# One gate-projection slot per attention head, another split of the modulation columns, and 32 bytes of padding

## What is computed

```python
# first block
h = rms_norm(x, g_pre)
mla_in, rwkv_in, z_mla, z_rwkv, gate_mla, gate_rwkv = split(h @ w_in)
q, kv = ...                      # latent projections, rms norm, rotary part
y_mla = mla_attention(q_nope, q_rope, k_nope, k_rope, v_mla)   # 8 heads, softmax over 256 keys
y_rwkv = bidirectional_scan(...)                               # 16 heads = 8 pairs
# each y is multiplied by z * sigmoid(z); then branch projections, gates, w_out, residual
# third block, from the vector c alone
mod = silu(c) @ w_ada + b_ada    # 6 * 2048 values = 96 columns of 128
```

## Time and profile before

| | |
|---|---|
| median of 3 runs | 3726.21 us (3722.5 to 3728.68) |
| the profiled execution's own time | 3726.89 us |
| its span, first to last instruction | 3725.6 us |
| PE busy | 3562.8 us (96%) |
| DVE busy | 2231.9 us (60%) |
| ACT busy | 1407.4 us (38%) |
| mean granted TensorE clock | 0.984 of full |
| DMA | 654.13 MB, mean 176 GB/s |

### The profile page before, as it was taken

The page is one execution under the profiler, slowest core; times in us unless marked ns, Lnnn a source line. Parts: engine busy times, 40 slices in busy tenths (PEclk is TensorE's granted clock), DMA queues, the critical chain, the costliest instruction groups (busy, mean ns, idle before and its releaser), DMA issues.

```text
span 3725.6 us, 63401 instructions
## 1 busy us (share of the span) xinstructions
PE 3562.8 (96%) x26060; PEld 3360.3 (90%) x26060; DVE 2231.9 (60%) x3036; ACT 1407.4 (38%) x1686; POOL 76.1 (2%) x155
## 2 busy tenths in 40 slices
PE   8998899999999999989999999998998899999998
PEld 8996688888888886789999999988988899999998
DVE  7775455555446569765555554545566677777544
ACT  5441132332320000554444433335355444445443
POOL 0001100000000100000000000000000000000000
PEclk9998999999999999989999999999999999999999
DMA  8657511111137984435555555543442455555554
GB/s 315 253 187 316 217 62 60 48 48 59 62 135 277 382 335 149 172 125 183 188 182 190 181 193 192 193 169 127 160 158 97 154 183 189 182 190 181 192 192 147
DMA packets 91728, 654.13 MB, mean 176 GB/s; under 512 B 10177, under 2 KB 10817, under 8 KB 13122
## 3 DMA queue, kind: packets, MB, share of 16 engines
q1 hardware_dynamic: 74736, 540.05, 40.1%
q0 software_dynamic: 14256, 103.82, 7.1%
q10 hardware_dynamic: 2594, 8.15, 0.6%
HBM read 649.88 MB, written 2.10 MB: 175 GB/s over the span
## 4 chain that ended last, share of the span: by engine, by line
PE 86%; DVE 7%; DMA 3%; ACT 3%; issue 1%; ACTq 0%; DVEq 0%
PE ps L442 19%; PE ps L444 19%; PE ps L443 19%; PE ps L414 8%; PE ps L603 6%; DMA work<-in_ada 3%; PE ps L677 2%; PE ps L665 2%; PE ps L473 1%; DVE work L1589 1%; PE ps L488 1%; DVE ring_parts L1574 1%; PE ps L721 1%; PE ps L712 1%; ACT work L1218 1%
## 5 line engine op out<-in xcount | busy, mean ns | idle before, releaser
L1574 DVE TENSOR_TENSOR ring_parts<-ring,ring_hi 128x1024 fp32r<-128x1024 f32 x810 | 976.5, 1224 | 787.9 <-ACT ring_hi L1054 777.8
L1054 ACT ACTIVATE ring_hi<-ring 128x1024 fp32r<-128x1024 f32 x810 | 852.8, 1061 | 1085.9 <-PE ps L444 1072.2
L443 PE MATMUL ps<-h_lo,ring_hi 128*128 128x256 f32 x2624 | 733.5, 280 | 0.0
L442 PE MATMUL ps<-h_hi,ring_hi 128*128 128x256 f32 x2112 | 596.4, 282 | 16.3 <-DVE ring_parts L1574 11.9
L444 PE MATMUL ps<-h_hi,ring_parts 128*128 128x256 f32 x2112 | 593.2, 281 | 0.0
L443 PEld LDWEIGHTS ps<-h_lo,ring_hi 128*128 128x128 f32 x2624 | 494.5, 188 | 1.3 <-issue 1.2
L442 PE MATMUL ps<-x_hi,ring_hi 128*128 128x256 f32 x1664 | 467.3, 281 | 5.8 <-DVE x_lo L1596 4.5
L444 PE MATMUL ps<-x_hi,ring_parts 128*128 128x256 f32 x1664 | 467.5, 281 | 0.0
L443 PE MATMUL ps<-x_lo,ring_hi 128*128 128x256 f32 x1664 | 463.6, 279 | 0.0
L442 PEld LDWEIGHTS ps<-h_hi,ring_hi 128*128 128x128 f32 x2112 | 398.3, 189 | 19.3 <-DVE ring_parts L1574 13.5
L444 PEld LDWEIGHTS ps<-h_hi,ring_parts 128*128 128x128 f32 x2112 | 399.1, 189 | 0.0
(11 more groups left out here) (422 smaller groups left out, 5418.9 us busy)
## 6 DMA issues: line engine op xcount, KB each, us to landing
ring<-in_weights SPq DMA_DIRECT2D x511, 1024.0 KB, 4.8
work<-in_ada POOLq DMA_DIRECT2D x96, 1024.0 KB, 8.9
work<-in_c_row POOLq DMA_DIRECT2D x3, 1024.0 KB, 5.2
resid<-in_lora ACTq DMA_DIRECT2D x9, 256.0 KB, 2.6
resid<-in_x SPq DMA_DIRECT2D x4, 512.0 KB, 6.3
resid<-in_x ACTq DMA_DIRECT2D x1, 2048.0 KB, 14.6
out<-work SPq DMA_DIRECT2D x4, 512.0 KB, 2.9
con<-in_const ACTq DMA_DIRECT2D x1, 1536.0 KB
```

The costliest lines, as they stand in the source:

```text
L442: mm(o, w_hi[:, k, cols], hi(kc), start=(kc == 0 and m % 2 == 0), stop=False, skip_group_check=True)
L443: mm(o, w_hi[:, k, cols], lo(kc), start=False, stop=False, skip_group_check=True)
L1054: A(high_ring(n)[:, 2 * (e % 2) + half, :], ring[:, n % RING, half * (SLOT // 2):(half + 1) * (SLOT // 2)], ACT.Copy)\
L1574: tt(lo, x, high_ring(n)[:, e % 4, :].bitcast(F32), ALU.subtract).then_inc(S("lo_ready"), 1)
```

## The change

Four things are changed. (1) `half_slot` does half of a weight slot: TensorE does one slot of z2 in each head g, the first half ahead of the wait for that head's probabilities and the second half between the transposes and PV. Group 0 is complete in g = 3 and group 1 in g = 7, so ScalarE's sigmoids and `gate_z` move there too; the second `gate_z` comes after all heads. (2) The runs of modulation columns are 16, 24 and 56 in place of 16, 28 and 52. (3) Ahead of the heads VectorE does 6 columns in place of 12, and behind the heads 3, 2, 2, 2, 3, 2, 2, 2. Of run 2 it does 6 and 6 in place of 4 and 4 at the first two places. (4) A pad of 8 floats (32 bytes) per partition ahead of the work area brings its start to a multiple of 512 bytes.

```diff
-ADA_RUNS = [16, 28, 52]
+ADA_RUNS = [16, 24, 56]
@@
+    pad = -(-(-nc.sbuf_base // 32) * 32) % 512 // 4
+    if pad:
+        sb("pad", [P, pad])
     work_at = -(-nc.sbuf_base // 32) * 32
+    assert work_at % 512 == 0
@@ tensor engine
+        def half_slot(n, half, rhs, b, k0, last):
+            ws = weights(n).rearrange("p (k c) -> p k c", k=KPS)
+            for k in (2 * half, 2 * half + 1):
+                kc = k0 + k
+                for m in range(4):
+                    ins = mm(PS[:, b + m // 2, (m % 2) * T:(m % 2 + 1) * T], ws[:, k, m * P:(m + 1) * P], rhs(kc),
+                             start=(kc == 0 and m % 2 == 0), stop=(kc == last - 1), skip_group_check=True)
+            if half == 1:
+                ins.then_inc(w_used, 1)
@@
             if hd >= 1:
                 g = hd - 1
+                z2_slot = lambda half: half_slot(slot0("z2") + g, half, h, 2 * PAIR["z2", g // 4][0], KPS * (g % 4), DC)
+                if g % 4 == 0:
+                    banks_free("z2", g // 4)
+                z2_slot(0)
                 t.wait(S("probs_ready"), 1)
@@
                 t.give(ins, S("pt_ready"))
-                if g in (2, 5):
-                    j = (g - 2) // 3
-                    by_feature(slot0("z2", j), 4, h, banks_free("z2", j))
+                z2_slot(1)
                 pe.wait_ge(S("pt_copied"), g + 1)
@@ scalar engine
-                if g in (2, 5):
-                    j = (g - 2) // 3
+                if g in (3, 7):
+                    j = g // 4
                     group_done("z2", j)
@@ vector engine
-        modulation(16, 12)
+        modulation(16, 6)
@@
-            if hd >= 1 and hd - 1 in (3, 6):
-                gate_z("z2", (hd - 1 - 3) // 3, 2 + (hd - 1 - 3) // 3)
+            if hd in (5, 9):
+                gate_z("z2", hd // 8, 2 + hd // 8)
@@
-                count = 5 if hd in (3, 6) else 1
-                modulation(28 + hd + 4 * (hd > 3) + 4 * (hd > 6), count)
+                modulation(22 + 2 * hd + (hd > 0) + (hd > 4), (3, 2, 2, 2, 3, 2, 2, 2)[hd])
@@
-        modulation(44, 4)
+        modulation(40, 6)
         first_branch(2)
         first_branch(3)
-        modulation(48, 4)
+        modulation(46, 6)
```

## The result

| | before | after |
|---|---|---|
| median | 3725.02 us (3722.5 to 3728.68, 4 runs) | 3681.27 us (3666.76 to 3698.78, 4 runs) |
| ratio to before, 95% interval | | 0.9884 [0.9839, 0.9928] |
| the profiled execution's own time, its span | 3726.89, 3725.6 us | 3678.85, 3677.5 us |

The change makes the kernel 43.7 us faster, where 26.2 were forecast and 36 was the best case of the range. The executions are also further apart: 32 us in four, where the kernel before spans 6 in its four here and 8 to 15 in the 15 to 27 executions beside each later experiment. The gain beyond the forecast and most of the spread come with one part, the pad.

A forecast was written before the change was run, and what follows sets the result against it. TensorE, busy 96% of the span, was taken as the bound, so gains lie where it idles or runs at low clock. Heads -33.5 and branch +6.6 sum to -26.9 us: 3700, range 3690 to 3711.

The forecast's parts named there:

- The step that failed: the pad: Padding ahead of the work area: no cost or gain on the engines, since nothing in the rows waits for an address.
- The heads: First scores to the scan's first matmul: 91.4 us in place of 124.9, 33.5 us less.
- the clock: First head: 1.5 us lost to a lower granted clock after TensorE's idle time.
- the tail's idle: After the last z2 matmul: sigmoid, second `gate_z` and the load into `LW` leave TensorE idle 4.4 us.
- that rival: VectorE paces the heads, columns at 3.84 us each with no slices landed ahead: 6.2 us late, 3706; chance 0.10.
- The branch after the scan: Two moved columns ahead of `first_branch(2)` make TensorE wait 5.1 us, plus 1.5 for the clock: 6.6 us more.
- loses nothing: After the scan, rival: the branch loses next to nothing, 1.9 us and no clock, 3694; chance 0.06.
- all four: After the scan, rival: all four moved columns fall on the chain, 15.4 us in place of 5.1, 3710; chance 0.06.
- The sum's wait: At the sum after the modulation columns, TensorE's wait of 2.24 us stays as before, only later.
- the rival on the aligned work area: Aligned slices land faster, the chain of 28 columns ends earlier, TensorE's 2.24 us wait goes: 3698; chance 0.04.
- The slower case: TensorE's clock stays at half through the heads: 3780; chance 0.05, of which 0.03 slower and 0.02 near no change.
- The bound on HBM reads: In the heads, HBM to SBUF bound near 358 GB/s makes three-column heads late, 4 us more, 3704; chance 0.03.

The follow-up runs named there:

- e3: The changed kernel timed once more with a second profile, nothing altered; 3674.18 us, 0.9859 of the kernel before.
- e2: The whole change without its pad, against the kernel before; 3699.86 us, ratio 0.9929.
- e1: The kernel before with nothing but the 32-byte pad ahead of the work area; 3695.21 us, ratio 0.9927.
- e6: The kernel before with 96 bytes of padding ahead of the work area; 3734.45 us, ratio 1.0009.
- e9: The changed kernel without the pad, both half slots behind the transposes; 3712.93 us, 0.9973 of the kernel before.
- e11: The changed kernel without the pad, run 2's columns 4 ahead of the first branches, 6 behind, 6 after br_rwkv's second group; 3691.3 us, 0.9911 of the kernel before.
- e4: The kernel before with 32 bytes ahead of the weight ring, so ring and work area move together; 3723.2 us, ratio 0.9994.
- e12: The changed kernel, pad included, with run 2's columns spread as in e11; 3665.76 us, 0.9849 of the kernel before.
- e14: The kernel before with 32 bytes ahead of the ring and 32 ahead of the work area; 3695.43 us, ratio 0.9931.

## Why the prediction was right and where it failed

**The step that failed: the pad.** The prediction says "Cost and gain on the engines: nothing", with "The full-clock matmuls leave as little" as its reason for TensorE. Measured, the pad is worth 25.7 us on top of the plan (3674.18 of e3 against 3699.86 of e2; 21.0 with the eight executions of the changed kernel taken together, median 3678.86) and 29.8 alone (e1). The rows I had gave a matmul's time per element of one kind, the plain float32 ones, and these indeed do not move: 215.83 ns with and without. The split matmuls fill most of the span, and I read no row of them. Their 117.78 ns are what the engine takes in a chosen layout, and nothing in the rows showed it to be a floor. The reason given for VectorE was of the same sort: it compared a long and a short operand in one layout, and such a comparison cannot tell what another layout does. A chance for "spacing of the split matmuls changes" should have stood among the rivals, with both signs, since e6 shows that it can go up.

**The heads: right, −33.5 forecast, −32.6 in e2 by the scan** (−34.4 in e2 and −34.5 in after from the first scores to the scan, which is what the forecast summed: 90.6 and 90.5 us against 91.4). By the terms: idle ahead of the first transposes 3.96 us (4.3); the clock 5.14 − 3.45 = 1.7 (1.5); heads 9.94 apart (10.15, which counted 0.66 for the transposes where 0.44 was due); and the tail's idle 4.88 (4.4), since the load of `LW` landed after 3.2 us and not 2.6. That the difference came out within a microsecond is in part luck: the 124.9 us taken for the old heads is one trace, and the nine kernels that keep them took 119.2 to 125.4. The stretch was at 292 GB/s for a DMA share of 0.75, and VectorE waited 0.8 us in all for slices in it, too little to pace a head: that rival falls. The transposes wait in no later head, as said, and e9 shows what hid that wait (1.7 us a head without the half slot).

**The branch after the scan: right in place and near in size.** 6.6 us was charged (5.1 waiting, 1.5 clock). It was 5.67 of idle and, by e2's starts, 6.9 between scan and sum in all. In that number the sum's old wait has shrunk by 1.3; without this the loss is 8.2. The old kernels themselves take 861.5 to 865.5 us for that stretch from trace to trace, so the size is known to about 2 us. Where the columns stand was the cause: e11, which does two of them behind the branches and two later still, gets 5.8 back in that stage. The rival "loses nothing" falls, and so does "all four": no chain of 15 us is seen.

**The sum's wait.** It was forecast to stay ("the sum's wait of 2.24 included"). It is 0.9 in e2 and gone in after. Two readings are open: that the columns of that stage caught up with TensorE, which was late by the branch's wait, or that they ended earlier, as in the rival on the aligned work area. The wait is gone in e4 too, which has the old branch and the alignment.

**The slower case.** The clock stayed high through the heads (0.98), and e9 adds that it stays so (0.99) with 1.7 us of waiting in each head.

**Aligned slices.** From first start to last, the last 28 columns took 100.8 to 102.3 us in the five kernels whose work area starts at a multiple of 512, and 101.8 to 106.7 in the eleven where it does not. These overlap, but among the nine with the old heads the two aligned ones (e1 and e4) are the shortest, after and e3 are shorter than e2, and e12 is shorter than e11. In all five aligned kernels the sum's wait is gone, and among the unaligned with the old heads it is 0.5 to 3.5 us in six of seven. So the rival's mechanism, a chain of columns that ends earlier, is likely at work, though with one trace each it is not shown. It is no rival for the gain: e4, which has the alignment and nothing else, is at 0.9994 [0.9985, 1.0003].

**The bound on HBM reads.** The stretch of the changed kernel after the scan moves 428 GB/s with the DMA share at 1.01. That again is above the 358 GB/s that the Trainium skill (DMA: Bandwidth & Descriptors, "Where 436 GB/s comes from") gives for a core, and the 4 us that its rule would have cost did not appear: of the two heads with three columns the first ran them back to back, and the second is 9.94 us long like its neighbours. This kernel had one core at work, so its rows say nothing of cores that read at the same time.

**What stays open.** Why the byte distance between buffers changes the spacing of split matmuls, which operands decide in the stages other than block two's gated part, what chooses between the two values behind the wait, and what else sets the executions of the kernels with the pad apart.

## What to carry to other kernels

When an engine is busy all the time at full clock, its instructions' spacing is still not a floor: measure it per kind of instruction, from start to start, and try 32, 64 and 96 bytes of padding between the buffers that its operands come from before taking it as given. Judge such a trial with several executions, since here the layouts that changed the spacing in long stages spread over 13 to 45 us from one to the next. For engines that take turns, put independent work of the size of the partner's turn ahead of each wait, and when side work is moved out of one place, check every read that it now stands ahead of at the other: there it cost a fifth of what it had won.

## What the runs showed of the hardware

- Split matmuls (fp32r, 128x256, stationary operands alternating between buffers) start 117.78 ns apart in the old layout at full clock. With other distances between the ring and the work area, in steps of 32 bytes, it is 115.56, 118.89 or 119.1 ns in long stages, and 113.3 in short ones; plain float32 matmuls keep 215.83 ns.
- At one and the same distance it takes one of two values (115.56 or 117.78) for a whole feed-forward, from a wait inside it on (1.3 to 2.4 us long). The traces show it between kernels (115.56 in e1, e12 and e14, 117.78 in after and e3), not between executions of one. Kernels with that distance spread over 13 to 32 us in four to six executions; the kernel before over 8 to 15 in 15 to 27.
- Idling of 1.7 us in every 11.9 leaves the granted clock at 0.99, where 12 us of idling in 19 had been at 0.58.
